# Two operand tiles laid out anew: where each chunk of the normalised input and of the gated products begins in a partition

## What is computed

```python
def swiglu(x, w_gate, w_up, w_down):
    return (jax.nn.silu(x @ w_gate) * (x @ w_up)) @ w_down
...
    for l in range(DEPTH):
        h = h + 0.5 * swiglu(rmsnorm(h, ffn1_norm[l]), ffn1_w_gate[l], ffn1_w_up[l], ffn1_w_down[l])
        proj = rmsnorm(h, mix_norm[l]) @ w_in[l]
...
        h = h + jnp.concatenate([y_ret, y_diff], axis=-1) @ w_out[l]
        h = h + 0.5 * swiglu(rmsnorm(h, ffn2_norm[l]), ffn2_w_gate[l], ffn2_w_up[l], ffn2_w_down[l])
```

## Time and profile before

| what | value |
|---|---|
| device time, median of 3 runs | 2172.41 us (2171.02 to 2173.03) |
| the profiled execution's own time | 2171.49 us |
| its span, first to last instruction | 2169.4 us |
| mean granted TensorE clock | 0.999 of 2.4 GHz |
| TensorE busy / weight loads busy | 2158.6 / 2039.7 us |
| VectorE / ScalarE / GpSimd busy | 1559.8 / 1221.0 / 459.9 us |

### The profile page before, as it was taken

The page is one execution under the profiler, slowest core; times in us unless marked ns, Lnnn a source line. Parts: engine busy times, 40 slices in busy tenths (PEclk is TensorE's granted clock), DMA queues, the critical chain, the costliest instruction groups (busy, mean ns, idle before and its releaser), DMA issues.

```text
span 2169.4 us, 38708 instructions
## 1 busy us (share of the span) xinstructions
PE 2158.6 (100%) x15614; PEld 2039.7 (94%) x15614; DVE 1559.8 (72%) x2588; ACT 1221.0 (56%) x2017; POOL 459.9 (21%) x499
## 2 busy tenths in 40 slices
PE   9999999999999999999999999999999999999999
PEld 9999999999999999988988999889888999999888
DVE  8655876765665586886697586975876688887863
ACT  6444465544544446665566545654655676676652
POOL 1000522420341052232053000430331011101420
PEclk9999999999999999999999999999999999999999
DMA  8655434975796543565566554755565665674653
GB/s 278 206 167 172 154 125 133 236 195 172 190 214 175 184 156 117 162 207 184 166 210 199 192 178 156 233 184 187 192 195 175 171 193 169 178 235 142 225 178 105
DMA packets 424082, 395.35 MB, mean 182 GB/s; under 512 B 16816, under 2 KB 420400, under 8 KB 423905
## 3 DMA queue, kind: packets, MB, share of 16 engines
q1 hardware_dynamic: 410336, 375.22, 55.5%
q0 software_dynamic: 13280, 17.33, 4.0%
q10 hardware_dynamic: 288, 0.34, 0.0%
HBM read 389.20 MB, written 7.41 MB: 183 GB/s over the span
## 4 chain that ended last, share of the span: by engine, by line
PE 92%; DVE 4%; ACT 2%; DMA 1%; issue 1%; SPq 0%; DVEq 0%; ACTq 0%
PE ps L1672 29%; PE ps L1668 25%; PE ps L1670 16%; PE ps L1671 16%; DVE t L1163 1%; PE ps L2011 1%; PE ps L2012 1%; PE ps L2010 1%; PE ps L1687 1%; DMA t<-attn_w_qkv 1%; ACT t L836 0%; PE ps L1978 0%; PE ps L1962 0%; PE ps L1991 0%; ACT t L996 0%
## 5 line engine op out<-in xcount | busy, mean ns | idle before, releaser
L1672 PE MATMUL ps<-t 128*128 128x256 f32 (+1 forms) x5456 | 1548.2, 284 | 0.0
L1672 PEld LDWEIGHTS ps<-t 128*128 128x128 f32 x5456 | 1029.1, 189 | 0.1
L1163 DVE TENSOR_TENSOR t<-t 128x1024 fp32r<-128x1024 f32 (+1 forms) x722 | 877.2, 1231 | 172.9 <-ACT t L836 172.3
L1670 PE MATMUL ps<-t 128*128 128x272 f32 (+1 forms) x3036 | 876.0, 289 | 0.0
L836 ACT ACTIVATE t<-t 128x1024 fp32r<-128x1024 f32 (+1 forms) x722 | 730.0, 1030 | 258.2 <-PE ps L1672 231.8
L1671 PE MATMUL ps<-t 128*128 128x272 f32 (+1 forms) x3036 | 866.0, 285 | 0.0
L1668 PE MATMUL ps<-t 128*128 128x512 f32 x2420 | 840.2, 390 | 0.0
L1670 PEld LDWEIGHTS ps<-t 128*128 128x128 f32 x3036 | 571.5, 188 | 5.4 <-issue 3.0
L1671 PEld LDWEIGHTS ps<-t 128*128 128x128 f32 x3036 | 574.3, 189 | 0.9
L1668 PEld LDWEIGHTS ps<-t 128*128 128x128 f32 x2420 | 454.3, 188 | 95.0
L760 POOL TENSOR_TENSOR t<-t 128x256 f32<-128x256 f32 x110 | 100.4, 913 | 694.3 <-ACT t L954 694.3
(11 more groups left out here) (200 smaller groups left out, 1572.2 us busy)
## 6 DMA issues: line engine op xcount, KB each, us to landing
t<-ffn_w_in SPq DMA_DIRECT2D x88, 1024.0 KB, 5.3
t<-ffn_w_gate SPq DMA_DIRECT2D x42, 1024.0 KB, 5.6
t<-ffn_w_up SPq DMA_DIRECT2D x42, 1024.0 KB, 7.1
t<-attn_w_qkv SPq DMA_DIRECT2D x72, 512.0 KB, 5.0
t<-ffn_w_down SPq DMA_DIRECT2D x32, 1024.0 KB, 5.3
t<-ffn_w_out SPq DMA_DIRECT2D x32, 1024.0 KB, 5.2
t<-w_in SPq DMA_DIRECT2D x28, 1024.0 KB, 5.0
t<-ffn_w_down SPq DMA_DIRECT2D x16, 768.0 KB, 4.4
```

The source lines that it names most:

```text
L1163: dve.tensor_tensor(wlo[:, plan.place[n], 0:nk, :], kept(u)[:, 0:nk, half * P:half * P + P], f32(whi[:, plan.place[n], 0:nk, :]), ALU.subt ...
L1670: pe.matmul(o, hi, xhi, start=i == 0, stop=False)
L1672: ins = pe.matmul(o, lo, xhi, start=False, stop=i == r.nk - 1)
```

## The change

A small class holds a tile and, for each chunk, where its two parts start; `part(k, m, c0, c1)` cuts one part and `both(k)` gives the two as one operand of two rows.

```diff
+class Rows:
+    def __init__(self, whole, starts, n):
+        self.whole, self.starts, self.n = whole, starts, n
+    def part(self, k, m, c0, c1):
+        first = self.starts[k][m]
+        return self.whole[:, first + c0:first + c1]
+    def both(self, k):
+        first, second = self.starts[k]
+        return self.whole[:, first:first + 2 * (second - first)].rearrange("p (m c) -> p m c", m=2)[:, :, 0:self.n]
...
-        x = alloc(ctx, [P, KC, 2, T], F32R)
+        x_all = alloc(ctx, [P, X_ROOM], F32R)
...
-                a = alloc(region, [P, FCH, 2, T], F32R)
+                a_all = alloc(region, [P, FCH * 2 * T], F32R)
...
-        x_close, a_close, y_close = close(x, KC, HALF_LINE), close(a, FCH, HALF_LINE), close(y, KC, 0)
+        def spread(n, places, between):
+
+            starts, at = [], 0
+            for place in places:
+                while at % LINE != place:
+                    at += 1
+                starts.append((at, at + between))
+                at += between + n
+            return starts
+
+        x = Rows(x_all, spread(T, [0, 16, 32, 48, 8, 24, 40, 56], 320), T)
+        x_close = Rows(x_all, spread(SEQ, [0, 8, 16, 24, 32, 40, 48, 56], SEQ), SEQ)
+        a = Rows(a_all, [(2 * k * T, 2 * k * T + T) for k in range(FCH)], T)
+        a_close = Rows(a_all, spread(SEQ, [*range(0, 64, 4), 1, 3, 5, 6, 10, 11], SEQ), SEQ)
+        y_close = close(y, KC, 0)
...
-                act.activation(placed(e, parts_of(e)[:, m, 0, 0:T - c0]), hm, ACT.Copy, scale=gain(e, m)).then_inc(S["xh"], 1)
+                act.activation(placed(e, parts_of(e).part(m, 0, 0, T - c0)), hm, ACT.Copy, scale=gain(e, m)).then_inc(S["xh"], 1)
```

More of the change, by code:

```diff
@@ L30 @@
 HALF_LINE = 8
+LINE = 64
+X_ROOM = 4800
 NH = 16
@@ L752, in low_a @@
                     w.wait_ge(S["ah"], FCH * f + j + 1)
-                    pool.tensor_tensor(a_close[:, j, 1, :], us[:, j % 2, 0:SEQ], f32(a_close[:, j, 0, :]),
+                    pool.tensor_tensor(a_close.part(j, 1, 0, SEQ), us[:, j % 2, 0:SEQ], f32(a_close.part(j, 0, 0, SEQ)),
                                        ALU.subtract).then_inc(S["al"], 1)
@@ L936, in high_a @@
                     w.wait_ge(S["prod"], FCH * f + j + 1)
-                    act.activation(products_of(s)[:, j, 0, 0:N], us[:, j % 2, 0:N], ACT.Copy).then_inc(S["ah"], 1)
+                    act.activation(products_of(s).part(j, 0, 0, N), us[:, j % 2, 0:N], ACT.Copy).then_inc(S["ah"], 1)
                 def second(j, m, t):
@@ L1175, in low_x @@
                 w.wait_ge(S["xh"], KC * e + m + 1)
-                hi, lo = (parts_of(e)[:, m, i, 0:T - c0] for i in range(2))
+                hi, lo = (parts_of(e).part(m, i, 0, T - c0) for i in range(2))
                 dve.scalar_tensor_tensor(placed(e, lo), hm, gain(e, m), placed(e, f32(hi)), ALU.mult, ALU.subtract).then_inc(S["xl"], 1)
@@ L1616, in _ @@
             w.wait_ge(S["h0"], 16)
-            dve.tensor_scalar(x[:, 0, 0, :], h[:, 0, :], gain(0, 0), None, ALU.mult).then_inc(S["xh"], 1)
+            dve.tensor_scalar(x.part(0, 0, 0, T), h[:, 0, :], gain(0, 0), None, ALU.mult).then_inc(S["xh"], 1)
             for k in range(KC):
@@ L1679, in project @@
                 xs, first = parts_of(r.stage), start_of(r.stage)
-                matmuls(r, range(KC), lambda k, c0: (xs[:, k, 0, c0 - first:T - first], xs[:, k, 1, c0 - first:T - first]), ready, hook,
-                        both=(lambda k: x_close[:, k, :, :]) if STAGES[r.stage][0] == FFN and joined(r.stage)[0] else None)
+                matmuls(r, range(KC), lambda k, c0: (xs.part(k, 0, c0 - first, T - first), xs.part(k, 1, c0 - first, T - first)), ready, hook,
+                        both=x_close.both if STAGES[r.stage][0] == FFN and joined(r.stage)[0] else None)
             def project_first(r):
@@ L1686, in product @@
                     wt, m = ((whi, 0), (whi, 1), (wlo, 0))[part]
-                    return pe.matmul(ps[:, r.banks[j], 0:T], wt[:, plan.place[j], k, :], x[:, k, m, :],
+                    return pe.matmul(ps[:, r.banks[j], 0:T], wt[:, plan.place[j], k, :], x.part(k, m, 0, T),
                                      start=(part, k) == (0, 0), stop=(part, k) == (2, KC - 1))
@@ L1752, in ffn @@
                     if r.first - T0[s] >= 2 * FCH:
-                        matmuls(r, range(FCH), lambda k, c0: (products_of(s)[:, k, 0, 0:N], products_of(s)[:, k, 1, 0:N]), ready,
-                                both=(lambda k: a_close[:, k, :, :]) if halves(s, r) else None)
+                        matmuls(r, range(FCH), lambda k, c0: (products_of(s).part(k, 0, 0, N), products_of(s).part(k, 1, 0, N)), ready,
+                                both=a_close.both if halves(s, r) else None)
             def start_work():
@@ L2007, in values @@
                             hook[j](k)
-                            xhi, xlo = (x_close[:, k, m, j * P:(j + 1) * P] for m in range(2))
+                            xhi, xlo = (x_close.part(k, m, j * P, (j + 1) * P) for m in range(2))
                             hi, lo = (wt[:, p0:p0 + 3, k, :] for wt in (whi, wlo))
```

2 lines of the change are left out of this document (1 added, 1 removed).

## The result

The changed kernel takes 2184.65 us (median of 4 runs, 2184.16 to 2185.01) against 2172.23 for the kernel before (4 runs): a ratio of 1.0058, 95% interval 1.0046 to 1.0071. It is slower by 12.4 us. The forecast was 6.4 us faster.

What follows compares the result with a forecast made beforehand. TensorE was taken as the bound. Savings of 5.3 us in the feed-forwards and 1.1 in the mixers, other terms 0, made 6.4 us off the median 2172.4: 2166.0 us; own range 2164 to 2168, 8-in-10 range 2163 to 2187.

Steps and rivals of the forecast that it cites:

- What bounds the kernel: Whole kernel: TensorE busy 2158.6 of 2169.4 us, so the distance from one matmul's start to the next counts.
- the attribution to moves: 272-token matmuls: changing place costs 1.7 ns per matmul, about 5 ns per triple, through the way to the low part and back.
- rival (3): Place relative to the weights costs, not moving; 8 is good, others 1.5 to 1.7 ns a matmul; +9.7 us, 2182; chance 0.20.
- the step of 32 is free: Wide layout of 272 tokens: the move of 32 floats to the next chunk costs 0.
- The line of 123.7 ns: Straight line between 256 and 512 columns gives 272 columns 123.7 ns a matmul; the wide layout pays 1.8 ns more.
- The half share for the mixers: Mixers: half of 448 triples' 2.2 us counted as saved, 1.1 us, since the chain runs through weight splitting on DVE.
- New steps cost 0: Close 256-token layouts: new moves of +8 or mostly +4 per chunk cost 0, at most 5.5 us.
- Odd places: Six of 22 chunks of close `a` begin off the grid of 4 floats; cost taken as 0.
- The work called hidden: ACT, DVE and POOL writing the same runs elsewhere, and loads keeping up with TensorE: cost 0.
- (1): Every move costs 1.7 ns wherever it goes: wide `x` saves 4.3 us, close layouts pay 5.5; 2173.6 us; chance 0.19.
- (2): Place does not matter and the 1.7 ns have another cause; no change, 2172.4 us; chance 0.12.
- (4): Odd places break the stream: odd chunks of `a` at half or three-quarter rate add 26 to 51 us, 2198 to 2223; chance 0.07.

Runs made afterwards that it cites:

- wide_one: Kernel before, both parts of all 272-token input chunks at one place: 8 in first feed-forward and mixers, 0 in second, 24 in third; 2173.36 us, ratio 1.0008.
- steps2: Kernel before, 256-token chunks of five feed-forwards mixing places 8 and 40, 40 and 0, 8 and 0, or 56 down to 0; 2178.49 us.
- best3: Kernel before with 272-token input at 48, 256-token chunks and convolution products at 4, but dilated attention's input and last feed-forward at 8; 2160.32 us, ratio 0.9942.
- the map: Three runs of the kernel before, mostly one unchanging place per stage, together trying many places; 2185.72, 2181.9 and 2184.43 us.
- weights_moved: Kernel before with split weights 8 floats later, other tiles unmoved modulo 64, and constant places 16, 8, 24, 0, 32 in the 256-token feed-forwards; 2181.65 us.

## Why the prediction was wrong

**What bounds the kernel** was read rightly. TensorE is full in the feed-forwards before and after, nothing waits longer, and nearly all of the 12.4 us is the distance between matmuls.

**The failed step is the attribution to moves**, and it rests on two readings. The first is the earlier trace rows, twelve start-up matmuls at 123.6 ns, taken as "272 columns at an unchanging place go at the line's rate". `wide_one` has 272 columns at three unchanging places in full streams: 125.3 at 0, 125.7 at 8, 126.7 at 24. Twelve matmuls of the start didn't stand for a stream: in the run of after sixteen of the same line are (2.17 - 0.29) / 15 = 125.3 apart, and in `steps2`, which has the wide `x` at the very places of before, the same last twelve are (1.68 - 0.29) / 11 = 126.4 apart. So the earlier trace rows didn't repeat, and with it falls what it was held to say against rival (3). Timeline of PE, start-up, first after, then `steps2`:

```profile
5.72 2.17 PE L1717 MATMUL ps<-t 128*128 128x272 f32 x16
```

```profile
6.52 1.68 PE L1731 MATMUL ps<-t 128*128 128x272 f32 x12
```

The second is the earlier trace rows, 118.3 ns for 256 columns at changing places, read as a surcharge for change. Its high parts are at 16 and 48 and its low parts at 32 and 0, and each triple reads the high part twice, so their seats alone give (2 x 353.3 + 360.0 + 2 x 353.3 + 359.7) / 18 = 118.5. The row showed seats, and I compared it with place 8 without asking whether another unchanging place would also be at 116.6. No row of before could tell the two apart, since all its long unchanging streams are at 8; this should have kept rival (3) as likely as the forecast. That the step of 32 is free doesn't follow from the earlier trace rows either: the two streams compared there, `x` and `a` of 272 tokens, stand on the same four places.

**The line of 123.7 ns** for 272 columns was right in size: 370.0 / 3 = 123.3 at place 48. The 1.8 ns above it exist and can be had. They are had by a good place, not by leaving moves out: before's (0, 16)/(32, 48) and the changed kernel's eight places give the same 376.7, and `x` gained 0 where 5.3 us were put down. That the line came out so near is luck, as the earlier trace rows, its support, didn't repeat, and other unchanging places lie up to 3.0 ns a matmul above it. The half share for the mixers went with it, though `best3` shows that even half was too much: 0.8 of 3.0.

**"New steps cost 0"** failed with 11.9 us in the streams (some 12.7 with the dilated attention), above the 5.5 that was kept as the upper bound. That bound scaled the price of a move, and the cost is by the map mostly another thing: 2.9 of 4.0 ns a pair are seats. Nor was it right that place 8 is the least there is; for triples place 4 is 10 ns below.

**Odd places** were costed rightly at nothing here: pairs of `a`, with such chunks among their 22, take 350.58, no more than pairs of `x` without any. But that is no clean bill, since a stage wholly at 9 pays 10.0 ns a pair and 12.2 a triple over place 8. The Trainium skill's rule (SBUF — State Buffer, Specifications (TRN2)) that each step to a new 16-byte line has its price would make place 9 less than 1% dearer (an estimate from it, 129 lines for 128) and all multiples of 4 alike. Measured are 2.9% for 9, and 16, 24 and 48 lie on that grid and cost 2 to 7 ns a pair, so the rule alone doesn't describe what happens.

**The work called hidden** was hidden: DVE, ACT and POOL are busy as long as before within 1.2%, and the first of PE's waits is 1.4 us in both.

**The rivals.** (3), the seat, is the one that holds. Its 9.7 us had 1.5 ns for each of 6480 matmuls; measured are 4.0 / 2 = 2.0 in the pairs, 1.5 in the convolution and 2.1 in the triples of `a`, steps included. It said that all places but 8 are dear, which is too simple: 0, 12, 36 and 40 are as good for pairs. (1) is not refuted as a small share: about 1 ns a pair in the changed kernel is left for steps, and -1.7 to 6.3 elsewhere. (2), that the place doesn't matter, falls with the map, and with `weights_moved` falls its best reason: the Trainium skill (TensorE: Matmul & The Clock Gate, "What happens when you issue a matmul") gives the two reads ports of their own, by which moving the weights alone would leave the matmuls' distance as it was. It went from 350.0 to 359.7 ns a triple. (4) is refuted: no pair of `a` in the changed kernel takes over 364 ns.

The range, 2163 to 2187, held the 2184.65 only because rival (3) had been priced up to 14 us.

## What to carry to other kernels

When TensorE is full, the place where the streamed operand begins, counted modulo 64 floats from where the weights begin, was worth 2 to 6% of a matmul's distance here between multiples of 4 alone, and costs next to nothing to choose. It was tried only with float32r operands of 256 to 512 columns and new 128 x 128 weights for every matmul. Try a few unchanging places for each shape of stream in the real kernel (here 8 for pairs, 4 for triples of 256 columns, 48 for 272) before spreading chunks over many, and look at every stage of the result, since the same place can give two rates. And when a surcharge is read off the trace as the price of change, ask whether any row shows the same place without the change; where none does, seat and move are one number with two names.

## What the runs showed of the hardware that was not expected

The distance depends on the two operands' places relative to each other: five streams of triples moved with the weights' shift of 8 floats as the map says, within 0.2 ns. Triples of 256 columns range from 340.0 (place 4) to 366.6 ns (place 5), one float apart, triples of 272 from 370.0 (40, 44, 48) to 380.0 (16, 24), pairs from 346.7 to 356.7 (9); the columns alone take 320 and 340 at 2.4 GHz. And one stream at one place can run in either of two steady rhythms, 346.7 or 360.0 ns a pair at place 4 and 340.0 or 356.0 a triple, 349.8 or 346.7 a pair at 12, 350.0 or 353.3 a triple at 8, and pass from one to the other where a normalisation's two or more matmuls are put in between.
